# Channel mixer of a decoder trunk in three token passes, up and down projection both in seven block products

## What is computed

```python
    xp = xp + mp
    pn = _rmsnorm(xp, ln_mlp[l])
    xp = xp + jnp.square(jax.nn.relu(pn @ w_up[l])) @ w_down[l]
    y_prompt = _rmsnorm(xp, ln_final)[:, N_META:]
```

## Time and profile before

| what | value |
|---|---|
| median of 3 runs | 2339.76 us (2338.31 to 2340.43) |
| profiled execution, its own time | 2339.3 us |
| span of its instructions | 2337.5 us |
| PE busy | 2306.4 us (99%) |
| DVE, ACT, POOL busy | 1219.4, 810.4, 534.7 us |
| moved by DMA | 247.33 MB |

### The profile page before, as it was taken

How to read it: one execution, slowest core, us unless ns; L and a number is a source line. 1 busy time by engine, 2 the same in 40 slices (tenths; PEclk the granted TensorE clock), 3 DMA queues, 4 the chain that set the end, 5 groups by cost and what they waited for, 6 DMA issues and landing times.

```text
span 2337.5 us, 37069 instructions
## 1 busy us (share of the span) xinstructions
PE 2306.4 (99%) x15645; PEld 2082.8 (89%) x15645; DVE 1219.4 (52%) x2074; ACT 810.4 (35%) x1443; POOL 534.7 (23%) x408
## 2 busy tenths in 40 slices
PE   8999999999999999999999999999999999999998
PEld 6788788878877877888999999999999999999998
...
PEclk9999999999999999999999999999999999999999
...
DMA packets 86566, 247.33 MB, mean 106 GB/s; under 512 B 14465, under 2 KB 29953, under 8 KB 86401
## 3 DMA queue, kind: packets, MB, share of 16 engines
...
...
## 4 chain that ended last, share of the span: by engine, by line
PE 95%; DMA 1%; DVE 1%; ACT 1%; SPq 1%; issue 0%; POOL 0%; DVEq 0%; ACTq 0%
PE bank L772 23%; PE bank L774 23%; PE bank L773 23%; PE aux L1039 5%; PE aux L1041 5%; PE aux L1040 5%; PE bank L1039 1%; PE bank L1041 1%; PE bank L1040 1%; PE aux L966 1%; PE aux L874 1%; DMA kept_lo<-w_lo 1%; PE aux L937 1%; PE aux L907 1%; PE aux L936 1%; DVE hb L2060 0%
## 5 line engine op out<-in xcount | busy, mean ns | idle before, releaser
L772 PE MATMUL bank<-a_hi,w_hi 128*128 128x358 f32 (+3 forms) x1600 | 579.3, 362 | 9.4 <-DVE w_lo L1906 6.5
L774 PE MATMUL bank<-a_hi,w_lo 128*128 128x358 f32 (+3 forms) x1600 | 563.5, 352 | 0.0
L773 PE MATMUL bank<-a_lo,w_hi 128*128 128x358 f32 (+3 forms) x1600 | 562.7, 352 | 0.0
L772 PE MATMUL bank<-b_hi,w_hi 128*128 128x358 f32 (+4 forms) x1280 | 450.8, 352 | 3.5 <-POOL w_lo L699 3.5
L773 PE MATMUL bank<-b_lo,w_hi 128*128 128x358 f32 (+4 forms) x1280 | 451.2, 352 | 0.0
L774 PE MATMUL bank<-b_hi,w_lo 128*128 128x358 f32 (+4 forms) x1280 | 451.0, 352 | 0.0
L699 POOL TENSOR_TENSOR w_lo<-w_st,w_hi 128x1024 fp32r<-128x1024 f32 x86 | 209.2, 2433 | 806.9 <-ACT w_hi L1141 806.9
L1141 ACT ACTIVATE w_hi<-w_st 128x1024 fp32r<-128x1024 f32 x208 | 219.3, 1054 | 419.1 <-PE aux L1041 250.3
L772 PEld LDWEIGHTS bank<-a_hi,w_hi 128*128 128x128 f32 x1600 | 301.0, 188 | 40.5 <-DVE w_lo L1906 8.5
L704 POOL TENSOR_TENSOR w_lo<-w_st,w_hi 128x512 fp32r<-128x512 f32 x192 | 248.3, 1315 | 366.0 <-ACT w_hi L1141 366.0
L773 PEld LDWEIGHTS bank<-a_lo,w_hi 128*128 128x128 f32 x1600 | 301.4, 188 | 27.0 <-issue 1.7
...
## 6 DMA issues: line engine op xcount, KB each, us to landing
...
```

The source lines that it names most:

```text
L772: pe.matmul(ps, wh, xh, start=(j == 0), stop=False)
L773: pe.matmul(ps, wh, xl, start=False, stop=False)
L774: mm = pe.matmul(ps, wl, xh, start=False, stop=(j == 7))
```

## The change

- The channel mixer runs in three token passes, q = 0, 1, 2, each of two tiles of equal width w: 328, 352 and 360 tokens (`MW`). Pass q = 0 follows the token mixer of the first half; the 352 tokens that it leaves (`LEFT`) are made tile 0 of q = 1. They wait in DRAM (`x1_d`, `bn_d`) meanwhile.
- All 4096 hidden columns are in eight groups of 512, and the up projection is in seven products too: 2 blocks (j = 0, 1) of seven products with 4 steps of the contraction, then 4 blocks (j = 0 to 3) of seven products with 2 steps. There is no dense part left.
- A hidden block is now the sum of several products: DVE takes Z, Y and V from ACT's negated copy of X in `tmp` (`gather`), and the four quarters `hb` are made from that and single banks (`middle`, `quarters`).
- Since sums of inputs are rounded, the input is multiplied by `rs` and `ln_mlp` before the split (`normed`, `right_low`, `right_high`), in front of and in the first group of a pass; the inputs of q = 1 and 2 in part earlier (`left_norm`, `next_norm`).
- Weights come in halves of 512 columns, one for an up product and one for two down products, 28 in a group, in four places. `next_half` on ACT rounds the half four further on, once PE is done with the place.
- The weights' sums: 16 DMAs for each of eight groups, issued by GpSimd, those of groups 5 to 7 between its subtractions in the first channel-mixer pass (L872 to L898 of the changed kernel).
- Pass 1's sum of input squares moves from DVE to GpSimd; the sum of final squares of q = 0 and 1 comes later; the last norm covers two tiles of 360 at once.

The diff is cut to its core.

```diff
-SG = 6
-SBLK = 12
-SHID = 4
+GROUPS = 8
 PAIRS = 4
-PROD = 7
+PASSES = 3
+HALVES = 28
+STREAM = GROUPS * HALVES
+UPS, PRODUCTS = 14, 42
 QW = 2 * P
-COPIES = 8 * SG
...
+MW = [328, 352, 360]
...
+X, Z, Y, V_ = range(4)
+BANK = {1: X, 5: Z, 7: Y, 6: V_, 2: X, 3: Y, 4: Z}
+OPENS = (1, 5, 7, 6)
+ORDER = [1, 5, 7, 6, 2, 3, 4]
+RIGHT = {1: 0, 6: 1, 7: 2, 5: 3, 2: 4, 3: 5, 4: 6}
 B11, T2, T3, T1, B21, B22, T4 = range(7)
...
+    up_sums = nc.dram_tensor("up_sums", [GROUPS, 4, 2, P, HW], F32, kind="Internal").ap()
+    down_sums = nc.dram_tensor("down_sums", [GROUPS, 4, PAIRS, P, QW], F32, kind="Internal").ap()
+    x1_d = nc.dram_tensor("x1_d", [KB, P, TH[0] + TH[1]], F32, kind="Internal").ap()
+    bn_d = nc.dram_tensor("bn_d", [KB, P, MW[1]], F32, kind="Internal").ap()
...
+            def split_half(h):
+                pool.wait_ge(w_split, MLP0 + h + 1)
+                pool.tensor_tensor(w_place(w_lo, h), w_place(w_st, h), w_place(w_hi, h).bitcast(F32),
+                                   ALU.subtract).then_inc(w_ready, 1)
...
+            for h in range(STREAM):
+                if h % HALVES == UPS + 4:
+                    sum_steps(EARLY_SUMS + h // HALVES, EARLY_SUMS, GROUPS)
+                split_half(h)
...
+                def three(ps, h, c, right_hi, right_lo, start, stop):
+                    wh, wl = (w_place(w, h)[:, c:c + P] for w in (w_hi, w_lo))
+                    pe.matmul(ps, wh, right_hi, start=start, stop=False, skip_group_check=True)
+                    pe.matmul(ps, wh, right_lo, start=False, stop=False, skip_group_check=True)
+                    return pe.matmul(ps, wl, right_hi, start=False, stop=stop, skip_group_check=True)
...
+                def up_product(q, g, k):
+                    i, j = UP_SEQ[abreast(q, g)][k]
+                    h = half_no(q, g, k)
+                    b = BANK[i]
+                    if i == 2:
+                        pe.wait_ge(h_act, act_no(q, g, j, "s"))
+                    elif i == 3:
+                        pe.wait_ge(h_dve, dve_no(q, g, j, "sY"))
+                    elif i == 4:
+                        pe.wait_ge(h_dve, dve_no(q, g, j, "sZ"))
+                    elif g or q == 2:
+                        last = {X: 2, Z: 4, Y: 3, V_: 6}[b]
+                        pe.wait_ge(product_read, take_no(q if g else 1, (g - 1) % GROUPS, j + 2, last))
...
+                    half_split(h)
+                    ps = group_bank(q, j, b)[:, 0:MW[q]]
+                    for kb in range(4):
+                        if g == 0 and j == 0:
+                            pe.wait_ge(r_dve, rd_no(q, f"lo{RIGHT[i]}", kb))
+                        mm = three(ps, h, P * kb, *right(q, RIGHT[i], kb), kb == 0 and i in OPENS,
+                                   kb == 3 and i not in (1, 5, 7))
+                    mm.then_inc(product_done, 1)
...
+                def down_product(q, g, d):
+                    j, n = divmod(d, len(ORDER))
+                    i = ORDER[n]
+                    h = half_no(q, g, UPS + d // 2)
+                    b = BANK[i]
+                    if i in OPENS:
+                        if j >= 2:
+                            pe.wait_ge(product_read, take_no(q, g, j - 2, {X: 2, Z: 4, Y: 3, V_: 6}[b]))
+                        elif b == X:
+                            pe.wait_ge(h_act, act_no(q, g, j, "r11"))
+                        else:
+                            pe.wait_ge(h_dve, dve_no(q, g, j, {Z: "c21", Y: "c12", V_: "sV"}[b]))
+                    else:
+                        pe.wait_ge(product_read, take_no(q, g, j, {2: 1, 3: 7, 4: 5}[i]))
+                    half_split(h)
+                    ps = group_bank(q, j % 2, b)[:, 0:MW[q]]
...
+                def next_half(q, g, at):
+                    h = half_no(q, g, at) + 4
+                    if h < (3 * STREAM if q else STREAM):
+                        round_half(h)
...
+                def up_stage(q, g):
+                    special = abreast(q, g)
+                    for j in range(2):
+                        k0 = 7 * j
+                        if not special:
+                            front(q, g, j)
+                            for k in range(4):
+                                next_half(q, g, k0 + k)
+                        middle(q, g, j)
+                        first_quarter(q, g, j)
+                        at = (8 + 3 * j) if special else k0 + 4
+                        next_half(q, g, at)
+                        next_half(q, g, at + 1)
+                        differences(q, g, j)
+                        next_half(q, g, at + 2)
+                        last_quarter(q, g, j)
+                        if j:
+                            next_half(q, g, UPS)
+                        fourth(q, g, j)
...
+                def gather(q, g, j, i):
+                    s_ = tmp[:, j, 0:MW[q]]
+                    dve.wait_ge(product_done, up_no(q, g, i, j))
+                    if i == 5:
+                        squared(q, g, j, "s")
+                    else:
+                        own(q, g, j, {7: "sZ", 6: "sY"}[i])
+                    step(tt(s_, s_, group_bank(q, j, BANK[i])[:, 0:MW[q]], ALU.subtract))
+                def middle(q, g, j):
+                    squared(q, g, j, "hi5")
+                    step(low(q, B22, j, hb(q, 2), -1.0))
+                def quarters(q, g, j):
+                    w = MW[q]
+                    h11, h12, h22, h21 = (hb(q, i) for i in range(4))
+                    s_ = tmp[:, j, 0:w]
+                    squared(q, g, j, "q11")
+                    step(low(q, B11, j, h11))
+                    dve.wait_ge(product_done, up_no(q, g, 3, j))
+                    step(stt(h12, group_bank(q, j, Y)[:, 0:w], -1.0, s_, ALU.mult, ALU.subtract))
+                    own(q, g, j, "c12")
+                    step(stt(h12, h12, 0.0, h12, ALU.max, ALU.mult))
+                    own(q, g, j, "r12")
+                    step(tt(h11, h11, h12, ALU.subtract))
+                    step(tt(h12, h22, h12, ALU.subtract))
+                    dve.wait_ge(product_done, up_no(q, g, 4, j))
+                    step(tt(h21, group_bank(q, j, Z)[:, 0:w], s_, ALU.add))
+                    squared(q, g, j, "hi3")
+                    step(low(q, T1, j, h11))
+                    squared(q, g, j, "hi2")
+                    step(low(q, T3, j, h12))
+                    own(q, g, j, "lo3")
+                    step(stt(h22, h22, -1.0, h11, ALU.mult, ALU.subtract))
+                    if j:
+                        take(q, g, 0, 1)
+                    squared(q, g, j, "q21")
+                    squared(q, g, j, "hi1")
+                    step(low(q, T2, j, h22))
+                    step(low(q, B21, j, h21))
+                    if j:
+                        take(q, g, 0, 5)
+                        take(q, g, 0, 7)
+                    step(tt(h21, h21, h22, ALU.add))
+                    squared(q, g, j, "hi6")
+                    step(low(q, T4, j, h21))
+                def take(q, g, j, i):
+                    x11, x12, x21, x22 = quadrants(q, j)
+                    dst, op = {1: (x22, ALU.subtract), 5: (x22, ALU.subtract), 7: (x22, ALU.subtract),
+                               6: (x22, ALU.subtract), 2: (x11, ALU.add), 3: (x12, ALU.subtract),
...
+                def up_stage(q, g):
+                    for j in range(2):
+                        for i in (5, 7, 6):
+                            gather(q, g, j, i)
+                        middle(q, g, j)
+                        quarters(q, g, j)
...
+                        takes(q, g, j)
+                        if q == 0 and g in (2, 3):
+                            left_norm(4 * (g - 2) + j)
+                        elif q == 1 and 2 <= g < 6:
+                            next_norm(4 * (g - 2) + j)
+                        elif (q, g) == (1, GROUPS - 1):
+                            if j == 0:
+                                dve.wait_ge(next_normed, 2 * KB)
+                                right_steps(2, ("lo0", 0), ("lo0", 3))
+                                right_steps(2, ("t3", 0), ("t3", 3))
+                            elif j == 1:
...
```

1388 lines of the change are left out of this document (809 added, 579 removed).

## The result

The changed kernel takes 2574.06 us (median of 4 runs, 2572.13 to 2580.31) against 2339.85 us for the kernel before on the same chip: a ratio of 1.1007, 95% interval 1.0987 to 1.1026. Slower was the likeliest sign in the forecast; the size was 99 us there and is 234 us here, 74 us above the top of the range. The profiled execution has a span of 2570.2 us, 232.7 more than before.

A forecast was written before the change was run, and what follows sets the result against it. PE, busy for 99% of the span, was taken to bound the kernel. -142 + 140 + 70 + 15 + 6 + 6 + 4 = +99 us on the profiled 2339.3 gave 2438 us; the range was 2285 to 2500.

The forecast's parts named there:

- matmuls removed: Channel mixer on PE: 2688 matmuls a pass at 0.455 ns a column, 1278 us in place of 1419.6: -142 us.
- steady waits, 21 groups: Groups after each pass's first: PE waits 7.3, 6.5 or 6.2 us a group because GpSimd's subtractions hold DVE: +140 us.
- first groups: First group of each pass: inputs normalised, rounded and combined first; 34 us without holding, 87 with; taken +70 us.
- extra steps in other groups: Four groups of q = 1, two of q = 2: four more two-SBUF-input DVE steps per output block; 0 to 25, taken +15 us.
- sums' DMAs: Pass q = 0: GpSimd issues 48 DMAs between subtractions, 0.62 us each; 0 to 15, taken +6 us.
- turn to the second mixer: Pass 1's token mixer starts only when the last product has left `dense`, its first rounding 8 x 0.58 us; taken +6 us.
- tail: Last scaling, at the end: 16 steps of 0.5 us in place of 8 in 4.06 us, on the path: +4 us.
- The doubt about 328 columns: Pass q = 0: if weight loads set the pace, matmuls would keep to 163 ns, 35 us more.
- The hold: DVE steps with two SBUF inputs and GpSimd subtractions (1.27 us) exclude each other; PE waits 6.5 us a group at 352.
- Rival A: Channel-mixer groups: subtractions rarely hold DVE, 0.8 us a group, so the products' gain stays: -79 us, 2260 us; chance 0.21.
- Rival C: PE's granted clock also falls after new waits in 21 groups and first groups: 48 us more, 2486 us; chance 0.12.
- the small terms: Extra DVE steps, the sums' DMAs, the turn and the tail: +15, +6, +6 and +4 us, range 18 to 52.

The follow-up runs named there:

- e5: Changed kernel with the 48 DMAs of the weights' sums left out and GpSimd subtracting only 8 of 512 columns of each weight half: 2360.15 us.
- e1: Changed kernel without the 48 DMAs of the weights' sums of groups 5 to 7, which read the sums of groups 2 to 4 instead: 2514.10 us.
- e2: Changed kernel with GpSimd subtracting only 8 of the 512 columns of each weight half, the others left out: 2407.38 us.
- e13: Changed kernel with ACT making the final squares of q = 1 one or two weight roundings earlier in the first group of q = 2: 2560.17 us.
- e14: Changed kernel with two of the change of basis's eight steps ahead of each pass's first take, six behind block j = 1's last quarter: 2569.00 us.
- e12: Changed kernel with 54 more, overwritten matmuls on PE in the long wait of each pass's first group: 2569.39 us.
- e4: Changed kernel with the same 48 DMAs of the weights' sums issued one by one, one behind every second subtraction: 2530.72 us.
- e6: Changed kernel with the seven additions of the second token mixer's input squares moved back from GpSimd to DVE: 2562.88 us.

## Why the forecast had the sign and missed the size

The terms of the sum, against the windows of the changed kernel (all its groups, not only those shown):

| term | forecast | measured | how |
|---|---|---|---|
| matmuls removed | -142 | not contradicted | e5: 51.3, 54.1, 55.8 us a group |
| steady waits, 21 groups | +140 | +126 | 7.0, 5.5 and 5.5 us a group |
| first groups | +70 | +130 | 45, 39 and 46 us over matmuls |
| extra steps in other groups | +15 | +27 | 12, 13 and 2 us |
| sums' DMAs | +6 | +51 (e1: 60, with group 0's) | groups 1 to 4 of q = 0 |
| turn to the second mixer | +6 | +37 | 23 in the last group, 14 in the mixer |
| tail | +4 | +8 | 19.2 us behind PE's last product, 11.3 before |

The start of the program is 3 us shorter. With rounding, the measured column adds up to the 375 us of PE's longer matmuls and waits. Of the 134 us by which the forecast was short, 60 are in the first groups, 45 in the sums' DMAs, 31 at the turn, 12 in the extra steps and 4 in the tail; the steady waits were 14 less than forecast.

- **Matmuls: right.** 337 matmuls in 54.23 us are 161 ns each at 352 columns. The doubt about 328 columns falls: 338 in 50.94 us, 151 ns, in e5.
- **The hold: right in kind and nearly in size**, from two places of the trace before. The two places at which PE waits were as stated; the first wait had its size, the second about half of it. Rival A (the gain stays) falls with e2: even with nearly all of the subtractions gone the kernel takes 2407 us.
- **The first groups: the step that failed by most, +70 forecast and +130 measured.** The mechanism was on the list, the count was too low, and not for the hold: I had 34 us without the hold, and e5 measured 85. Part of it is the circle of ACT's squares and DVE's additions in q = 2 (e13: 14 us), which I had priced as DVE's own time only, under the extra steps. The change of basis in front of the chain is worth 5 (e14), the clock 5 (e12). Of what is left, e5 shows only that it is in part PE's waits and in part matmuls at the lower clock (31 of the 85 us), which the count had not in it; I can't split it further, and its cause stays open: no run took the normalising of the inputs out, since the buffers would have been read unwritten.
- **The sums' DMAs: a step that failed, +6 forecast and +51 measured (e1: 60).** I priced the time to issue them, 0.62 us each. That held for the 12 of group 1, behind which PE waited 4.0 us; but the 14 of group 2 took GpSimd 18.6 us instead of 8.7, and PE waited 14.0. And I put the loads of weight halves beside them at nothing, where their median landing rose from 2.1 to 5.1 us and one took 14.4. e1 and e4 show what the DMAs cost, not how it divides between the two.
- **The turn: failed too, +6 forecast and +37 measured.** "Its sums of squares on GpSimd lie beside 20 us of PE work" held before, where they were DVE's and PE waited at most 1.1 us there. The instruction queued ahead of them on GpSimd, the reload, waits for PE's last product. e6 gives 11 us of the 37, and a wait of 10.7 us stays with it. Of the 14 us in the mixer, 7.6 are waits of PE and 7.1 longer matmuls. The 8.8 us for which ACT waits there for a weight half while the inputs are loaded was seen only in the chain and not tested.
- **Rival C (the clock): half right.** In ordinary groups, with waits of 1.0 to 2.6 us, the mean clock of a group stayed at 1.00 or 0.97. In the first group of q = 1 it stood at 0.50 to 0.60 behind waits of 2.6 and 9.7 us (1534 to 1538 and 1548 to 1556), and in group 1 of q = 0 at 0.58 behind one of 4.0 us. Of PE's extra busy time of 135 us, 74 are in the three first groups and in groups 1 to 4 of q = 0; the rival had spread its 48 us over all groups. e12 kept the clock up in three places and gained 5 us; what the clock costs in the others was not tested.
- **The extra steps and the tail.** +15 and +4 became +27 and +8. The last scaling was priced rightly (16 steps in 8.1 us); left out were DVE's additions of the last squares ahead of it, for which PE waits 3.3 us.
- **The range** ended at 2500 because the small terms had been bounded one by one from the nearest row of the same engine, and not by what waits behind them. Its 18 to 52 us for them is also not the sum of their own bounds, which give 4 to 56; that is small beside the miss.
